# Expert stage of a two-part transformer: dots against xn in PSUM, all v rows by TensorE, 20 row slots, projections one head ahead

## What is computed

```python
def peer(xn, w_q, keys1, keys2, u, v):          # T = 256 tokens, 8 heads, 128 keys, top 16
    q = (xt @ w_q).reshape(T, PEER_HEADS, 2, PEER_HALF)
    s1 = jnp.einsum('thd,nd->thn', q[:, :, 0], keys1)
    s2 = jnp.einsum('thd,nd->thn', q[:, :, 1], keys2)
    v1, i1 = lax.top_k(s1, PEER_TOPK)
    v2, i2 = lax.top_k(s2, PEER_TOPK)
    cand = (v1[..., :, None] + v2[..., None, :]).reshape(T, PEER_HEADS, 256)
    sc, ci = lax.top_k(cand, PEER_TOPK)
    experts = ...                                # 8 * 16 = 128 of 16384 experts per token
    gates = jax.nn.softmax(sc, axis=-1)
    ub = jnp.take(u, eb, axis=0)                 # one row of 1024 per token and expert
    hb = jax.nn.gelu(jnp.einsum('tkd,td->tk', ub, xb), approximate=False)
    vb = jnp.take(v, eb, axis=0)
    return jnp.einsum('tk,tkd->td', gb * hb, vb)
```

## Time and profile before

| what | value |
|---|---|
| runs before: median (lowest to highest) | 4304.86 us (4293.77 to 4305.95) |
| the profiled execution, its own time | 4303.91 us |
| its span in the trace | 4302.2 us |
| TensorE's granted clock over the span | 0.862 of full speed |
| PE busy; DVE busy; ACT busy; POOL busy | 3126.3 us; 2554.4 us; 1103.2 us; 1263.1 us |
| DMA: moved in all | 940.88 MB, mean 219 GB/s |
| first expert stage, first gather issued to last | 2466.8 to 3255.2 us |
| second expert stage, first gather issued to last | 3496.2 to 4284.7 us |

### The profile page before, as it was taken

The page is one execution under the profiler, slowest core; times in us unless marked ns, Lnnn a source line. Parts: engine busy times, 40 slices in busy tenths (PEclk is TensorE's granted clock), DMA queues, the critical chain, the costliest instruction groups (busy, mean ns, idle before and its releaser), DMA issues.

```text
span 4302.2 us, 45142 instructions
## 1 busy us (share of the span) xinstructions
PE 3126.3 (73%) x17054; PEld 2425.1 (56%) x17054; DVE 2554.4 (59%) x4443; ACT 1103.2 (26%) x1509; POOL 1263.1 (29%) x1110
## 2 busy tenths in 40 slices
PE   7999999989998799999999753433337783333334
PEld 6987999869896598997986441111114561111111
DVE  4554555555544555554543587777764458777776
ACT  3333333233331333334332211111101221111110
POOL 0000000000000000000000067777872027777776
PEclk9999999989999999999999786777678787767766
DMA  5523555435453345552452279999997049999998
GB/s 187 197 108 132 177 181 178 150 103 176 165 192 123 110 147 181 179 208 88 153 177 98 96 268 345 347 347 353 343 373 273 0 163 350 342 344 352 358 350 331
DMA packets 415039, 940.88 MB, mean 219 GB/s; under 512 B 27889, under 2 KB 210193, under 8 KB 414865
## 3 DMA queue, kind: packets, MB, share of 16 engines
q0 software_dynamic: 150048, 546.37, 34.7%
q1 hardware_dynamic: 259744, 390.09, 26.8%
q10 hardware_dynamic: 5072, 2.12, 0.2%
HBM read 937.45 MB, written 1.05 MB: 218 GB/s over the span
## 4 chain that ended last, share of the span: by engine, by line
PE 56%; POOL 24%; issue 9%; DVE 5%; DMA 5%; ACT 1%; ACTq 0%; SPq 0%; DVEq 0%; POOLq 0%
POOL wide_ring L2074 23%; PE bank L624 13%; PE bank L625 13%; PE bank L626 13%; DMA wide_ring<-in_peer_v,pk_idx 4%; PE bank L689 4%; PE bank L668 4%; PE bank L674 1%; PE bank L1001 1%; DVE xn L1432 1%; DVE x_lo L1448 1%; PE bank L704 1%; PE bank L837 0%; DVE resid L1469 0%; ACTq L1027 0%
## 5 line engine op out<-in xcount | busy, mean ns | idle before, releaser
L1001 PE MATMUL bank<-wide_ring,xT 128*128 128x512 f32 x960 | 548.6, 707 | 934.1 <-DMA wide_ring<-in_peer_v,pk_idx 933.9
L624 PE MATMUL bank<-x_hi,wide_hi 128*128 128x256 f32 x3328 | 958.2, 288 | 20.4 <-DVE x_lo L1448 20.0
L625 PE MATMUL bank<-x_lo,wide_hi 128*128 128x256 f32 x3328 | 954.6, 287 | 0.0
L626 PE MATMUL bank<-x_hi,wide_lo 128*128 128x256 f32 x3328 | 954.0, 287 | 0.0
L1001 PEld LDWEIGHTS bank<-wide_ring,xT 128*128 128x128 f32 x960 | 193.5, 221 | 1286.5 <-issue 1278.0
L1321 DVE TENSOR_TENSOR wide_lo<-wide_ring,wide_hi 128x2048 fp32r<-128x2048 f32 x228 | 522.0, 2289 | 493.0 <-ACT wide_hi L1094 493.0
L2057 POOL TENSOR_TENSOR small<-small,minus_half 128x1 f32<-128x1 f32 (+2 forms) x41 | 27.6, 673 | 2622.4 <-DVE small L1455 2276.9
L2074 POOL DMA_INDIRECT wide_ring<-in_peer_u,pk_idx x512 | 625.4, 1221 | 252.3 <-issue 135.3
L624 PEld LDWEIGHTS bank<-x_hi,wide_hi 128*128 128x128 f32 x3328 | 652.7, 196 | 28.9 <-DVE x_lo L1448 24.2
L625 PEld LDWEIGHTS bank<-x_lo,wide_hi 128*128 128x128 f32 x3328 | 652.7, 196 | 2.6
L626 PEld LDWEIGHTS bank<-x_hi,wide_lo 128*128 128x128 f32 x3328 | 651.9, 196 | 0.0
(11 more groups left out here) (271 smaller groups left out, 3798.1 us busy)
## 6 DMA issues: line engine op xcount, KB each, us to landing
wide_ring<-in_ffn_w_gate_up SPq DMA_DIRECT2D x176, 1024.0 KB, 9.5
deep_ring<-in_ffn_w_down SPq DMA_DIRECT2D x88, 1024.0 KB, 5.0
wide_ring<-in_sb_w_qkv SPq DMA_DIRECT2D x12, 2048.0 KB, 12.4
wide_ring<-in_w_in SPq DMA_DIRECT2D x12, 2048.0 KB, 10.1
wide_ring<-in_peer_w_q SPq DMA_DIRECT2D x8, 2048.0 KB, 12.4
wide_ring<-in_moba_w_qkv SPq DMA_DIRECT2D x6, 2048.0 KB, 12.2
deep_ring<-in_sb_w_o SPq DMA_DIRECT2D x8, 1024.0 KB, 8.3
deep_ring<-in_w_out SPq DMA_DIRECT2D x8, 1024.0 KB, 7.6
```

The lines of the kernel that those rows point to most:

```text
L624: mm(o, w[0], x[0], start=start, stop=False, skip_group_check=True)
L625: mm(o, w[0], x[1], start=False, stop=False, skip_group_check=True)
L626: return mm(o, w[1], x[0], start=False, stop=stop, skip_group_check=True)
L1001: ins = mm(acc[t][h][:, :], pk_diag[:, s % 2, k], row_at(ph, n)[:, h * 512:(h + 1) * 512], start=first, stop=last, skip_group_check=True)
```

## The change

- `ROWSLOTS` goes from 16 to 20: slots 0 to 3 are four rows in `deep_ring` (free once `mix2`'s output projection is done), slots 4 to 19 the old ones. Gather k uses slot k % 20 and waits for the use of row k-20.
- ACT copies `xn` of tile 0 to banks 2 and 3 before the first copy of queries, and `xn` of tile 1 to banks 4 and 5 once all queries are copied; the dots read `xn` from there. In the steps 0 to 7 the banks 2 and 3 are not yet needed for tile 1's sum.
- In steps 0 to 13 all 16 v rows go to PE, in steps 14 and 15 eight of them (before: 8, and 4). ACT makes as many diagonal matrices more; these lie in `arena` now.
- PE makes the queries of head h before the key scores of head h-1. The copies of queries go from DVE to ACT.
- DVE's order at the stage's start: pick 0 in two parts around the split of head 2, pick 1 around the split of head 5, the split of head 7 ahead of dot 3, pick 2 two stages at a time in the second half of step 0.

The diff, cut to its core:

```diff
+WIDEROWS = GSLOTS * KT * GCOLS // D
+DEEPROWS = DSLOTS * DROWS // P
+ROWSLOTS = DEEPROWS + WIDEROWS
 def on_tensor(step):
-    return range(1, BURST, 2) if step < STEPS - 2 else range(1, BURST, 4)
+    return range(BURST) if step < STEPS - 2 else range(1, BURST, 2)
-        pk_diag = xT[:].rearrange("p c t -> p (c t)").rearrange("p (b n m) -> p b n m", b=2, n=BURST // 2)
+        pk_diag = cut(14336, 2, BURST, P)
+        pair = [ctx.enter_context(nc.psum_tensor(f"pair{i}", [P, D], F32)) for i in range(4)]
+        bank = [pair[i // 2][:, (i % 2) * 512:(i % 2 + 1) * 512] for i in range(8)]
...
+                queries(0)
+                key_scores(0)
+                queries(1)
+                for h in range(2, PK_HEADS):
+                    queries(h)
+                    key_scores(h - 1)
+                key_scores(PK_HEADS - 1)
...
+                act.wait_ge(S["resid"], at["resid"])
+                A_(pair[1][:], xn[:, 0], ACT.Copy).then_inc(S["xn_copied"], 1)
+                def copy_q(h):
+                    act.wait_ge(S["wide"], at["wide"] + h + 1)
+                    act.wait_ge(S["key_scores"], PK_HEADS * i + max(h - 1, 0))
+                    A_(pk_q[:, h % 2].rearrange("p m t -> p (m t)"), work[h % 2][:, :],
+                       ACT.Copy).then_inc(S["wide_read"], 1)
...
+                copy_q(0)
+                copy_scores(0)
+                next_split(0)
+                for h in range(1, PK_HEADS):
+                    next_split(h)
+                    copy_q(h)
+                    if h > 1:
+                        copy_scores(h - 1)
+                    if h in (1, 4):
+                        gates(h // 4)
+                copy_scores(PK_HEADS - 1)
+                act.wait_ge(S["wide_read"], at["wide_read"] + 8)
+                A_(pair[2][:], xn[:, 1], ACT.Copy).then_inc(S["xn_copied"], 1)
...
                 def dot(s, n):
+                    row = ROW_NUMBER["u", s, n]
+                    if n == 0 and s % PK_HEADS == 0:
+                        dve.wait_ge(S["xn_copied"], TT * i + s // PK_HEADS + 1)
+                    await_row(dve, ph, row)
-                    V.tensor_tensor_reduce(out=row_at(ph, n), in0=row_at(ph, n), in1=xn[:, s // PK_HEADS],
+                    V.tensor_tensor_reduce(out=row_at(ph, row), in0=row_at(ph, row), in1=pair[1 + s // PK_HEADS][:],
...
                 split_head(1)
-                copy_q(0)
+                pick(0, 0, 4)
                 split_head(2)
-                pick(0)
-                copy_q(1)
+                pick(0, 4, PICK_STAGES)
                 split_head(3)
-                pick(1)
-                copy_q(2)
                 split_head(4)
+                pick(1, 0, 7)
+                split_head(5)
+                pick(1, 7, PICK_STAGES)
+                split_head(6)
                 for s in range(STEPS):
                     for n in range(BURST):
+                        if s == 0 and n == 3:
+                            split_head(7)
                         dot(s, n)
-                        if s + 2 < STEPS and n < PICK_STAGES:
+                        if s == 0 and n >= BURST // 2:
+                            pick(2, 2 * n - BURST, min(2 * n - BURST + 2, PICK_STAGES))
+                        if 0 < s < STEPS - 2 and n < PICK_STAGES:
                             pick_stage(ph, s + 2, n)
...
+                for k, (table, s, n) in enumerate(ROWS):
+                    if table == "u" and n == 0:
                         pool.wait_ge(S["pick_stage"], PICK_STAGES * (STEPS * i + s + 1))
+                    if k < DEEPROWS:
+                        pool.wait_ge(S["deep"], mixer["deep"] + 4)
+                    elif k < ROWSLOTS:
+                        pool.wait_ge(S["wide_lo"], ph.at["wide_lo"] + 2 * ((k - DEEPROWS) // 4 + 1))
+                    else:
+                        name, count = ROW_AFTER[ROWS[k - ROWSLOTS]]
+                        per = ROWS_USED if name == "row_used" else ROWS_MIXED
+                        pool.wait_ge(S[name], per * i + count)
```

91 lines of the change are left out of this document (46 added, 45 removed).

## The result

| what | value |
|---|---|
| changed kernel: median (lowest to highest) | 4200.68 us (4194.19 to 4201.56) |
| kernel before, beside it | 4304.86 us (4293.77 to 4305.95) |
| ratio of the changed kernel to the one before | 0.9759, 95% interval 0.9745 to 0.9772 |
| its profiled execution; its span | 4201.22 us; 4199.4 us |
| forecast | 4078 us, 4045 to 4200 |

The account below looks back on a forecast made before the run. The prediction took POOL's gather issue, stretched by DVE instructions with two SBUF operands, to bound the expert stages, with transfers next. 4303.9 - 182 (steady) - 48 (starts) + 4.6 (ends) = 4078.5, given as 4078 us, range 4045 to 4200.

Parts of the forecast that it names:

- steady parts: Gathers 52 to 511 of both expert stages: 1.297 us a gather instead of 1.495, 182 us less in both.
- starts: Gathers 0 to 51 of each expert stage: 24 us less a stage, 48 in both.
- all the rest: The forecast's term for the ends of both expert stages: 2.3 us more a stage, 4.6 in both.
- What held the gathers: Steady part: a gather waits for DVE instructions with two SBUF operands, not with one in PSUM; 933 ns against 1210.
- The steady step: 32 gathers in an expert stage's steady part: 41.5 us instead of 47.9, ends 40.6 and 43.5.
- The transfers: Steady part: next bound once POOL is freed, 42.3 or 40.5 us a step at 397 or 414 GB/s.
- The transfers are at their limit: Rival for the steady part: 366 GB/s at most, 45.8 us a step, 4204 us in all; chance 0.07.
- the forecast's 33.5 us a step: Steady part: PE's time for 16 v rows a step, fitting under 41.5 us with 8 us to spare.
- The slower rival: Steady part: PE stays at the low clock through a burst, 57.4 us a step, 4527 us in all; chance 0.04.
- The end: End of each expert stage: last row goes to PE at 3.59 us instead of DVE at 1.28, 2.3 us more.
- Slots: Steady part: waiting for PE's use of rows leaves 5 us to spare with 20 slots, none with 16.

Follow-up runs that it names:

- hold18_sem18: The changed kernel's 20 slots, with gather k waiting for the use of row k-18 and landings counted on 18 semaphores; 4067.8 us, ratio 0.9479.
- xn_sbuf: The changed kernel with the dots reading `xn` in SBUF again; 4189.8 us, ratio 0.9758.
- head_only: The changed kernel with 16 slots, `xn` for the dots in SBUF and half of the v rows on DVE again; 4268.7 us, ratio 0.9910.
- slots16: The changed kernel with the old 16 slots, none in the output panels' store; 4069.1 us, ratio 0.9483.
- group 6: Three runs on one chip crossing 18 or 20 slots with 18 or 20 landing semaphores, or shifting semaphore numbers; 4067.8, 4065.3 and 4066.4 us.
- v_half: The changed kernel with half of the v rows added by DVE again; 4092.0 us, ratio 0.9524.
- slots18: The changed kernel with 18 slots, 2 of them in the output panels' store; 4068.1 us, ratio 0.9486.
- group 7: One kernel, the changed one with 20 slots in its first expert stage and 18 in its second; 4209.4 us, ratio 0.9800.
- hold18: The changed kernel's 20 slots with gather k waiting for the use of row k-18; 4196.8 us, ratio 0.9759.
- group 2: Runs on one chip of the changed kernel with half the bytes, 16 slots, `xn` in SBUF, or half the v rows on DVE; 4032.1 to 4189.8 us.
- groups 1, 3 and 5: The changed kernel's first comparison, its repeat and the run with three parts undone, and four variants of slots or waits; 4193.1 to 4268.7 us.
- 2, 4 and 6: Groups of variants of the changed kernel in bytes, slots, parts undone, waits or semaphores, without the changed kernel itself; 4032.1 to 4398.4 us.

## Why the prediction was right or wrong

The sum of hold18_sem18 against the profiled execution before (4302.2 to 4064.7, 237.5 us less), and of the changed kernel (102.8 less), from the windows, in us:

| term | forecast | without pauses | changed kernel |
|---|---|---|---|
| steady parts | -182 | -98.6 - 98.0 = -196.6 | -28.6 - 29.7 = -58.3 |
| starts | -48 | -23.9 - 24.8 = -48.8 | -18.5 - 19.4 = -37.9 |
| all the rest | +4.6 | +7.9 | -6.6 |
| sum | -225.4 | -237.5 | -102.8 |

- **What held the gathers: right.** The median gather went from 1210 to 941 ns, and xn_sbuf, which undoes this one part, has it at 1164 for u rows. That DVE's instructions with one operand in PSUM leave POOL alone could be read from a single pair of lines.
- **The steady step: the failed step.** The forecast's 41.5 us a step took POOL to wait for nothing but transfers and slots, and put any other wait between gathers at nothing. Where that holds, it is 41.0 us (587.84 / 459 x 32). In the measured group it was 45.8, because POOL idled 82 us a stage beyond its 0.30 us, 69 us more than in hold18_sem18, in waits for increments that came late. This term stood in neither the sum nor the rivals, and why increments come late stays open. Nothing in the trace of before shows such a wait: its pauses between gathers are 0.30 us, and head_only, whose steady part is that of before (684.5 us), had no pause in a group that has them.
- **The transfers.** Taken at 40.5 to 42.3 us a step from short windows at 397 and 414 GB/s. Over 588 us they held 406 GB/s. The reading of a short undisturbed window was good for a long one. The share of 0.96 at 367 GB/s in the changed kernel is no limit: the same bytes pass at 1.02 and 406, and in the changed kernel itself at 409 and 411 GB/s right up to a pause and into it.
- **The rival that seems to have won.** "The transfers are at their limit" gave 1.433 us a gather and 4204 us, and the measured values are 1.433, 1.429 and 4200.7. It is refuted all the same, by slots16 and all of group 6, which move the same bytes in 1.28 us a gather. A number that agrees is no evidence for the mechanism that gave it. By the Trainium skill's figure ("DMA: Bandwidth & Descriptors", section "Where 436 GB/s comes from", about 358 GB/s) 4230 was estimated; 406 GB/s over two stretches of 588 us speaks against that limit in this kernel.
- **The start: right.** 24 us a stage, of which head_only shows 13 as the order of the heads; xn_sbuf shows 8 as the PSUM operand (86.0 us for 78.1), slots16 shows 2 as the slots (80.0), and the rows on PE bring none (76.1 in v_half). Gather 52 comes 78.06 us after gather 0 in hold18_sem18, where some 78 were forecast. In the changed kernel it is 83.5 us, since increments come late there too.
- **PE.** Busy 419 of 588 us at a granted clock of 0.86; the forecast's 33.5 us a step had room. The clock does fall to 0.50 while PE waits between two bursts (2765 to 2770 us in hold18_sem18, with 0.04 us of work), but within a burst it is back at 1.00 some 5 us in. The slower rival (0.04) was not near.
- **The end.** The two stretches behind a last gather, to the second stage's first gather and to the end, grew by 4.5 and 7.6 us in hold18_sem18 (245.5 for 241.0, 25.1 for 17.5), 12 where 4.6 were forecast; the first stage's first gather came 4.2 us earlier. The queue in front of the last gather is deeper now: the median landing takes 9.7 us, and it took 6.2.
- **Slots.** The forecast counted on 20 slots to keep POOL free and found no spare with 16. Measured, 16 slots, 18, and 20 held as 18 are 4069, 4068 and 4068 us where there are no pauses. The spare time was right only as far as it didn't matter: POOL is held a little (18 us a stage with 16 slots, 12 with 18) and loses nothing by it, since the transfers, at 406 GB/s, are the slower of the two. The changed kernel with all 20 slots in use and nothing else altered was not measured without pauses.

The range ended at 4200 because I cut off what lay above as the transfers' rival. It should have been wider: a kernel that issues more per microsecond met waits here that the slower kernel's trace doesn't have.

No version tried beats the changed kernel with certainty. slots18 and hold18_sem18 took 4068 us where there were no pauses, and 18 slots in a stage (group 7) or their holding (hold18) were of no use where there were. Not tried: v_half in a group with pauses. It has half of PE's rows and kept nine tenths of the gain in group 2 (0.0476 of 0.0517 of the time before), so it may well be the safer kernel.

## What to carry to other kernels

Repeat the kernel itself in every group of experiments. I ran the changed kernel in two groups of seven, both with pauses, and built several theories on a difference that lay between the groups. Where kernel and chip can't be crossed, put both variants in one kernel, as two stages of it: group 7 settled in one run what six groups had not. And when a forecast's mechanism shows in the trace (gathers at 0.94 us) but its time doesn't, look for idle time that ends with "remote" before doubting the mechanism. Look up which semaphore is waited for, and compare the time of its increment with the end of the instruction that makes it.

## What the runs showed of the hardware

- A gather's issue on POOL takes 0.94 us under a DVE instruction with one operand in PSUM and up to 1.9 us behind one that reads two in SBUF. The Trainium skill, "SBUF — State Buffer", section "Who interferes with whom", says that a DVE instruction with two SBUF inputs contends with a GpSimd instruction that reads SBUF, and infers that descriptor generation is spared. The prediction drew on the second of these alone. A gather reads its indices in SBUF, and its issue isn't spared: xn_sbuf against slots16 shows 121 us of the whole kernel.
- Gathers of 128 rows of 4 KB hold 406 GB/s for 588 us on one core; with at most four of them under way they fall to 322.
- In four of seven groups semaphore increments came late by microseconds, and POOL stood for 1.5 to 7.2 us at a time, 45 to 52 times a run (not in head_only), while records of increments and landings went missing. In the other three every increment of `pick_stage`, `row_used` and `row_mixed` lies within 0.015 us of its instruction's end. The medians of the kernel before (4303 to 4305 us in groups 1, 3 and 5, 4284 to 4296 in 2, 4 and 6, but 4296 in group 7) don't tell the two kinds of group apart.
